# MLP up tiles in a float32 kernel: the upper weights meet both input parts in one 512-column matmul, the halves are added on eviction, and GpSimd scales

## What is computed

```python
def _rmsnorm(x, g):
    y = x32 * lax.rsqrt(jnp.mean(x32 * x32, axis=-1, keepdims=True) + EPS)
    return y.astype(x.dtype) * g

def _sqrelu_mlp(h, w1, w2):          # w1: 1024 x 4096, w2: 4096 x 1024
    return jnp.square(jax.nn.relu(h @ w1)) @ w2
...
    x = x + _sqrelu_mlp(_rmsnorm(x, norm_mlp_g_2[i]), mlp_w1_2[i], mlp_w2_2[i])
```

## Time and profile before

| what | value |
|---|---|
| median of 3 runs | 2934.55 us |
| profiled execution, its own time | 2934.22 us |
| its span in the trace | 2932.4 us |
| TensorE matmul busy | 2793.4 us, 95% |
| VectorE busy | 1748.8 us, 60% |
| ScalarE busy | 1188.4 us, 41% |
| GpSimd busy | 197.3 us, 7% |
| memory traffic | 443.74 MB, mean 151 GB/s |

### The profile page before, as it was taken

The page is one execution under the profiler, slowest core; times in us unless marked ns, Lnnn a source line. Parts: engine busy times, 40 slices in busy tenths (PEclk is TensorE's granted clock), DMA queues, the critical chain, the costliest instruction groups (busy, mean ns, idle before and its releaser), DMA issues. The chain is left out here.

```text
span 2932.4 us, 45676 instructions
## 1 busy us (share of the span) xinstructions
PE 2793.4 (95%) x17786; PEld 2486.5 (85%) x17786; DVE 1748.8 (60%) x2269; ACT 1188.4 (41%) x1717; POOL 197.3 (7%) x224
## 2 busy tenths in 40 slices
PE   6999999789999999999879988999999999998998
PEld 4888876578887788888769988999999999998998
DVE  4776242557772377522655559765476577559764
ACT  4232232543222232322454455544554445455543
POOL 0000012000000000000200013000200000003000
PEclk8999999999999999999999999999999999999999
DMA  6555225025553245432225643565455556553553
GB/s 249 187 181 176 95 86 179 1 80 190 184 185 107 86 154 184 157 103 98 103 105 179 193 148 97 166 193 167 147 168 190 170 188 210 192 165 101 168 190 129
DMA packets 120374, 443.74 MB, mean 151 GB/s; under 512 B 13440, under 2 KB 14848, under 8 KB 119616
## 3 DMA queue, kind: packets, MB, share of 16 engines
q1 hardware_dynamic: 119248, 431.38, 45.1%
q0 software_dynamic: 1008, 10.75, 1.0%
HBM read 441.03 MB, written 1.05 MB: 151 GB/s over the span
## 5 line engine op out<-in xcount | busy, mean ns | idle before, releaser
L1596 DVE TENSOR_TENSOR wlo<-raw,whi 128x1024 fp32r<-128x1024 f32 x672 | 827.2, 1234 | 653.0 <-ACT whi L1142 650.1
L1142 ACT ACTIVATE whi<-raw 128x1024 fp32r<-128x1024 f32 x672 | 706.7, 1054 | 711.9 <-PE ps L498 636.0
L496 PE MATMUL ps<-nh,whi 128*128 128x512 f32 (+1 forms) x1696 | 621.3, 366 | 22.5 <-DVE nl L1661 18.1
L497 PE MATMUL ps<-nl,whi 128*128 128x512 f32 (+1 forms) x1696 | 615.2, 363 | 0.0
L498 PE MATMUL ps<-nh,wlo 128*128 128x512 f32 (+1 forms) x1696 | 614.6, 362 | 0.0
L496 PE MATMUL ps<-bh,whi 128*128 128x256 f32 x1664 | 482.0, 290 | 9.0 <-DVE bl L1683 7.5
L497 PE MATMUL ps<-bl,whi 128*128 128x256 f32 x1664 | 472.0, 284 | 0.0
L498 PE MATMUL ps<-bh,wlo 128*128 128x256 f32 x1664 | 471.7, 283 | 0.0
L496 PEld LDWEIGHTS ps<-nh,whi 128*128 128x128 f32 x1696 | 324.8, 192 | 93.0 <-issue 35.6
L498 PEld LDWEIGHTS ps<-nh,wlo 128*128 128x128 f32 x1696 | 324.6, 191 | 49.2
L497 PEld LDWEIGHTS ps<-nl,whi 128*128 128x128 f32 x1696 | 325.1, 192 | 47.2 <-issue 0.2
(11 more groups left out here) (223 smaller groups left out, 3206.9 us busy)
## 6 DMA issues: line engine op xcount, KB each, us to landing
raw<-stream SPq DMA_DIRECT2D x800, 512.0 KB, 3.4
head<-stream SPq DMA_DIRECT2D x8, 1024.0 KB, 15.2
gates_w<-gate_in POOLq DMA_DIRECT2D x2, 3328.0 KB, 12.4
cst<-cst_in POOLq DMA_DIRECT2D x2, 1280.0 KB, 5.9
X<-x_in SPq DMA_DIRECT2D x1, 2048.0 KB, 7.9
out<-X SPq DMA_DIRECT2D x8, 128.0 KB, 2.0
fftw<-fftw_in POOLq DMA_DIRECT2D x2, 256.0 KB, 5.9
ws<-ws_in POOLq DMA_DIRECT2D x1, 512.0 KB, 4.2
```

The lines of the kernel that those rows point to most:

```text
L496: pe.matmul(dst, w1, rhs_hi, start=start, stop=False)
L497: pe.matmul(dst, w1, rhs_lo, start=False, stop=False)
L1142: act.activation(whi[:, at % RING, :], raw[:, n % RING, :], ACT.Copy).then_inc(w_hi_ready, 1)
L1596: dve.tensor_tensor(wlo[:, r, :], raw[:, PLACE["main", at] % RING, :], whi[:, r, :].bitcast(F32), ALU.subtract).then_inc(w_ready, 1)
```

## The change

`bh` and `bl`, the upper and lower parts of the input, become two halves of one tensor `b2`, so that one matmul can take block k of both. A new `wide_tile` makes a tile from 16 matmuls: for each block, one of 512 columns (upper weights by upper and lower input) and one of 256 (lower weights by upper input, added to the first half). The tile fills a bank: columns 0 to 255 hold the upper-input sums, columns 256 to 511 those of the lower input. A unit so takes two banks, 0 and 1 for even units, 2 and 3 for odd ones. ScalarE copies the second halves of both banks to `tmpa`, VectorE adds the first halves to it (this now signals `up_evac`), then after its next split VectorE makes max(z, 0) * z in `tmpb`, GpSimd multiplies it by `inv_row` in place (`mlp_scaled`), and ScalarE's copy to `mh` waits for that. In the down stage, `first_two` asks for unit 14's release before banks 0 and 1 (12 products of three matmuls come before unit 15's release is asked for, 14 before the change).

```diff
-        bh = sb("bh", [P, KD, S], F32R)
-        bl = sb("bl", [P, KD, S], F32R)
+        b2 = sb("b2", [P, 2, KD, S], F32R)
+        bh, bl = b2[:, 0, :, :], b2[:, 1, :, :]
...
+            def wide_tile(b, at, dyn, first=False):
+
+                weights(at, dyn)
+                r = at % RING
+                for k in range(KD):
+                    if first:
+                        pe.wait_ge(nl_ready, c["nl"] - KD + k + 1)
+                    w1 = whi[:, r, k * P:(k + 1) * P]
+                    w2 = wlo[:, r, k * P:(k + 1) * P]
+                    if k < KD - 1:
+                        pe.matmul(bank(b), w1, b2[:, :, k, :], start=(k == 0), stop=False)
+                        pe.matmul(bank(b, S), w2, bh[:, k, :], start=False, stop=False)
+                    else:
+                        pe.matmul(bank(b, S), w2, bh[:, k, :], start=False, stop=False)
+                        last = pe.matmul(bank(b), w1, b2[:, :, k, :], start=False, stop=True)
+                last.then_inc(slots_done, 1)
...
# TensorE, first_two of the down stage
-                    for m in (2, 3, 4, 5, 6, 7, 0):
+                    for m in (4, 5, 6, 7, 0, 1):
                         mm3(bank(m, w), at + k, m, src_h(k, 0), src_l(k, 0), k == 0, False)
                 pe.wait_ge(up_evac, c["unit"] + 2)
                 for k in range(2):
-                    mm3(bank(1, w), at + k, 1, src_h(k, 0), src_l(k, 0), k == 0, False
-                        ).then_inc(slots_done, 1)
+                    for m in (2, 3):
+                        last = mm3(bank(m, w), at + k, m, src_h(k, 0), src_l(k, 0), k == 0, False)
+                    last.then_inc(slots_done, 1)
...
# ScalarE, unit
                 if mlp:
-                    act.activation(tmpa[:, u % 2, :], ps[:, u % 2, :], ACT.Relu).then_inc(up_act, 1)
+                    b = 2 * (u % 2)
+                    act.activation(tmpa[:, u % 2, :].rearrange("p (h t) -> p h t", t=S), ps[:, b:b + 2, S:T],
+                                   ACT.Copy).then_inc(up_act, 1)
...
                 if between:
                     between()

-                act.wait_ge(up_evac, udyn + (u + 3))
+                if mlp:
+                    act.wait_ge(mlp_scaled, udyn + (u - c["ffn_units"] + 1))
+                else:
+                    act.wait_ge(up_evac, udyn + (u + 3))
                 act.activation(dst[:, bass.ds(ldyn * w + local * w, w)], tmpb[:, u % 2, 0:w],
                                ACT.Copy).then_inc(hid_hi, 1)
...
# VectorE, unit
+                if mlp:
+                    b = 2 * (u % 2)
+                    z = tmpa[:, u % 2, :]
+                    halves_ = z.rearrange("p (h t) -> p h t", t=S)
+                    dve.wait_ge(up_act, udyn + (u + 1))
+                    dve.tensor_tensor(halves_, ps[:, b:b + 2, 0:S], halves_, ALU.add).then_inc(up_evac, 1)
+                    if between:
+                        between()
+                    dve.wait_ge(up_evac, udyn + (u + 3))
+
+                    dve.wait_ge(hid_lo, udyn + (u + 1))
+                    dve.scalar_tensor_tensor(out=tmpb[:, u % 2, :], in0=z, scalar=0.0, in1=z,
+                                             op0=ALU.max, op1=ALU.mult).then_inc(mlp_squared, 1)
+                    return
...
-                    dve.scalar_tensor_tensor(out=src, in0=ps[:, u % 2, :], scalar=0.0, in1=inv_row[:],
-                                             op0=ALU.max, op1=ALU.mult).then_inc(relu_scaled, 1)
-                    dve.wait_ge(relu_scaled, udyn + (u - c["ffn_units"] + 1))
...
# GpSimd, after the squares of each layer's MLP input
+                for u in range(NM // 2):
+
+                    if u == 0:
+                        pool.wait_ge(row_copied, c["cols"] - c["v"])
+                    pool.wait_ge(mlp_squared, c["mlp"] + u + 1)
+                    pool.tensor_tensor(tmpb[:, u % 2, :], tmpb[:, u % 2, :], inv_row[:], ALU.mult
+                                       ).then_inc(mlp_scaled, 1)
+                c["mlp"] += NM // 2
```

More of the change, by code:

```diff
@@ L320, in build @@
         row_copied = sem("row_copied")
-        relu_scaled = sem("relu_scaled")
         y_ready = sem("y_ready")
@@ L327, in build @@
         hid_hi = sem("hid_hi")
+        mlp_squared = sem("mlp_squared")
+        mlp_scaled = sem("mlp_scaled")
         hid_lo = sem("hid_lo")
@@ L577, in up4 @@
                         if mlp:
-                            dst = ps[:, u, half * S:(half + 1) * S]
+                            wide_tile(2 * u + half, at + 2 * u + half, dyn)
                         else:
-                            dst = bank(2 * u + half, w)
-                        src_h, src_l = (bh, bl) if mlp else (nh, nl)
-                        out_tile(dst, at + 2 * u + half, dyn, w, src_h, src_l)
+                            out_tile(bank(2 * u + half, w), at + 2 * u + half, dyn, w, nh, nl)
             def ada_streams(pair, even, odd):
@@ L668, in mlp_up @@
                 pe.wait_ge(up_evac, c["unit"] + 1)
-                out_tile(bank(0, S), at, 0, S, bh, bl, first=True)
-                out_tile(ps[:, 0, S:T], at + 1, 0, S, bh, bl)
+                wide_tile(0, at, 0, first=True)
+                wide_tile(1, at + 1, 0)
                 input_sums()
                 pe.wait_ge(up_evac, c["unit"] + 2)
-                out_tile(bank(1, S), at + 2, 0, S, bh, bl)
+                wide_tile(2, at + 2, 0)
                 input_rows(False)
-                out_tile(ps[:, 1, S:T], at + 3, 0, S, bh, bl)
+                wide_tile(3, at + 3, 0)
                 with pe.Fori(0, NM // 4 - 1) as i:
@@ L1428, in _ @@
             norm(S, split_out=False)
+            c["ffn_units"] = c["unit"]
             def b_upper(dst, m):
@@ L1734, in unit @@
             def unit(u, udyn, w, mlp, local, ldyn, between=None):
-                dve.wait_ge(up_act, udyn + (u + 1))
[L1737 to L1742, removed]
-                dve.wait_ge(hid_lo, udyn + (u + 1))
-                if mlp:
-                    dve.scalar_tensor_tensor(out=src, in0=ps[:, u % 2, :], scalar=0.0, in1=inv_row[:],
-                                             op0=ALU.max, op1=ALU.mult).then_inc(relu_scaled, 1)
-                    dve.wait_ge(relu_scaled, udyn + (u - c["ffn_units"] + 1))
-                dve.tensor_tensor(tmpb[:, u % 2, 0:w], tmpa[:, u % 2, 0:w], src, ALU.mult).then_inc(up_evac, 1)
+                if mlp:
[11 more added lines that the diff above has]
+                    return
+                dve.wait_ge(up_act, udyn + (u + 1))
+                dve.wait_ge(hid_lo, udyn + (u + 1))
+                dve.tensor_tensor(tmpb[:, u % 2, 0:w], tmpa[:, u % 2, 0:w], bank(2 * (u % 2) + 1, w),
+                                  ALU.mult).then_inc(up_evac, 1)
                 if between:
                     between()
-                if not mlp:
-                    lower(u, udyn, w, False, local, ldyn)
+                lower(u, udyn, w, False, local, ldyn)
             def lower(u, udyn, w, mlp, local, ldyn):
@@ L2034, in _ @@
                 residual(f"ffn2_down{l}", w, fix[:, 5 * l + 4, :, :])
-            c["ffn_units"] = c["unit"]
             norm_last("final1", lambda m: ("norm_mix", m))
@@ L2334, in _ @@
                     c["cols"] += 1
+                    c["v"] = 1
                 else:
```

## The result

The changed kernel takes 3028.51 us (median of 4 runs, 3026.77 to 3029.79), the kernel before 2932.52 us (median of 4): the ratio is 1.0324, 95% interval 1.0311 to 1.0337. It is slower by 96 us. The profiled execution took 3026.77 us with a span of 3025.0, 92.6 us more than the one before.

What follows compares the result with a forecast made beforehand. TensorE was taken to bound the kernel before, a ring of waits through three engines after. 2934.2 + 92 (four up stages at 23.0) - 1 (TensorE's quicker first tiles) = 3025 us; range 2995 to 3045.

Steps and rivals of the forecast that it cites:

- TensorE bounds the kernel before, with slack on the others: Up stages before the change: TensorE busy 93.8 of 94.5 us, 5.77 us a unit; ScalarE and VectorE have slack.
- The ring: Up-stage eviction: closed chain of waits through VectorE, GpSimd and ScalarE, 7.11 us per unit; chance 0.60.
- The port wait: GpSimd's product beside VectorE's line 1761: shared SBUF port costs 0.40 us per unit, bounds none to 0.46.
- the 86%: Share of GpSimd's time beside a two-input VectorE operation taken as lost: 0.85/0.99, from an earlier trace row.
- my 0.46: Time per unit that GpSimd's product and VectorE's line 1761 were expected to be at work together: 0.46 us.
- The case without a port wait: Rival: GpSimd and VectorE don't hinder each other in the up stage; 6.71 us a unit, 3003 us; chance 0.14.
- TensorE's saving is covered: Up stages: TensorE has 5.54 us of work per 7.11 us turn, stands still 1.57, so its saving gives nothing back.
- Its size: Saving from wide matmuls in up stages: 0.0136 us a block, 0.360 to 0.3464, 13.9 us over 1024 blocks.
- rival "faster": TensorE stays the up stages' bound, splits come in time and 13.9 us are gained: 2920 us; chance 0.08.
- The stage in order of time: Up stage followed unit by unit: down stage starts at 1976.2 instead of 1953.16, 23.0 us a stage, 92 for four.
- The clock: Rival: TensorE's pauses in each unit lower its granted clock and add to the loss; no price given; chance 0.02.

Runs made afterwards that it cites:

- ring opened: Changed kernel with ScalarE's copy to `mh` moved one unit later, behind the next unit's second ACT split: 2928.61 us, ratio 0.9990; second time 2929.51 us, 0.9986.
- first experiment: Changed kernel with TensorE's part undone, each block again three matmuls of 256 columns, eviction kept as changed: 3025.75 us, ratio 1.0327.
- five variants that keep the ring: Changed kernel with three narrow matmuls (3025.75 us), VectorE's product replacing GpSimd's (2966.81), subtraction moved (3004.43), squaring earlier (3004.23), or GpSimd's product halved (2994.97).
- four runs with the later copy: Changed kernel, `mh` copy one unit later: alone twice (2928.61, 2929.51 us), with `b2` laid out by block (2930.42), with matmuls grouped by size (2925.70).

## Why the prediction was right, step by step

Forecast 3025, measured 3028.5; forecast for the profiled execution +91, measured +92.6.

- **TensorE bounds the kernel before, with slack on the others: right.** With the ring opened, TensorE is the bound again.
- **The ring: right, 7.06 us against 7.11.** Its members, from the rows above: split to addition 1.15 (forecast 1.13), addition to split 0.60 (0.61), split to squaring 1.13 (1.13), squaring to GpSimd 0.76 (0.84, the one that was too long: I added the operation's full length and a handover of another pair of lines), GpSimd 1.67 (1.69), to ScalarE 0.15 (0.09), copy to split 0.53 (0.54), split to split 1.08 (1.08).
- **The port wait: right in kind, its size by luck.** 0.38 us against 0.40, shown by moving the neighbour away (1.29) and by putting a longer one there (2.20). But the 86% that I applied is not a rule: the loss is the shared time less 0.14 us, which would have made 0.32 of my 0.46. The two really share 0.52, because the handover before is shorter than I had it, and the two errors nearly cancel. The case without a port wait, 3003 us, was one of the two likeliest rivals; the kernel with the subtraction moved is that case in its ring (6.68 us against 6.71) and comes to 3004.4, though with a fall of the clock at each edge that my 3003 did not have.
- **TensorE's saving is covered: right** (first experiment). **Its size was wrong:** the step took 0.2264 us from a stream of wide matmuls alone, and in alternation with narrow ones they start 0.235 apart, the narrow ones 0.117. A block costs 0.352, not 0.346, so 1024 blocks give 8 us and not 13.9. The rival "faster" would so have been about 2926 rather than 2920; the two runs of the kernel with the later copy gave 2928.6 and 2929.5, with the 4.2 us of its four edges in them.
- **The stage in order of time: right.** 23.0 less 0.3 us a stage was the forecast; measured 22.1, 22.1, 21.0 and 22.1, 87.2 instead of 91. Most of the difference is the turn, thirteen times 0.05 us. The third is less because its stage was already 1.1 us longer before.
- **The clock: the step that was missing.** I expected down stages of 92 us as before; they are 94.3 to 94.9. I gave the clock a chance of 0.02 and argued from attention that pauses inside a unit would not lower it. That held: the wide tiles run at full clock. The fall comes at the edge, which the stage sum itself had: TensorE's last matmul of the up stage starts at 1967.23 and the first of the down stage at 1971.57, and matmuls of 256 columns then start 0.213 us apart until 1976.2, 0.120 after.

```profile
1967.23 0.39 PE L572 MATMUL ps<-b,whi 128*128 128x512 f32 x1
1971.57 0.58 PE L497 MATMUL ps<-mh,whi 128*128 128x256 f32 x1 [3.94 <-DVE wlo L1620]
...
1975.58 0.41 PE L497 MATMUL ps<-mh,whi 128*128 128x256 f32 x1
1975.79 0.41 PE L498 MATMUL ps<-ml,whi 128*128 128x256 f32 x1
...
1976.55 0.28 PE L499 MATMUL ps<-mh,wlo 128*128 128x256 f32 x1
1976.67 0.28 PE L497 MATMUL ps<-mh,whi 128*128 128x256 f32 x1
```

  With what follows the last one, the four down stages are 10.8 us longer. The fall belongs to the pause at the edge: in the changed kernel and the five variants that keep the ring, that pause is 3.34 to 4.34 us from last start to next, and at 23 of 24 edges the clock fell and the down stage was 1.3 to 2.8 us longer than 92.04; the exception is one of 3.34 us. In the traces of the four runs with the later copy it is 1.17 to 1.23 us, and at none of 16 edges did the clock fall. No run changes that pause alone. The 10.8 us made up for the 4 us that the up stages fell short and the 5.4 us that the rest of the span was quicker, so that the total came out nearer than its parts is luck.

## What to carry to other kernels

Before work goes to an idle engine, write out each engine's list and follow one item through it: a wait placed ahead of work that others need closes a ring, and the ring's length, not any engine's share, is then the pace. Here the shares were 93, 57, 39 and 10% in a kernel 3.2% slower. The cure was not a faster engine but one unit of distance: the waiting copy put behind the next unit's work. Then look at who shares a port with the moved work, since a wait for a port is booked as a longer instruction and not as a wait. And price a stall at a stage's edge twice, once for itself and once for the clock that may fall behind it.

## What the runs showed of the hardware beyond that

- Wide (512) and narrow (256) matmuls in alternation start 0.235 and 0.117 us apart, 0.352 a pair, where streams of one size give 0.2264 and 0.120, 0.346. One run or two runs of the moving operand made no difference. Changing size twice in a tile and not every time gave 0.230 and 0.119.
- GpSimd and VectorE with two SBUF inputs each hold the other up by what they share less 0.14 us, whichever came first: GpSimd's product goes from 1.29 to 1.67 and 2.20 us, VectorE's subtraction from 0.69 to 1.78 and its split from 1.22 to 2.31 us.
- A pause of TensorE of 4.34 us from the last start to the next at the edge of the stage was followed by a granted clock of 0.50 for the first 4.8 us of the next; with the ring open, the same edge had 1.17 us and no fall.
